# Four units of the second block's recurrent branch, computed in two parts around the end of the gather

## The reference

```python
# first block, last part: a product-key expert layer
u = expert_u[expert_idx]                       # 8 heads x 16 picks of 16384 experts, for each token
act = gelu(einsum('thkd,td->thk', u, hc))
vv = expert_v[expert_idx]
y = einsum('thk,thkd->td', gate * act, vv)
x = rmsnorm(x + y, final_g)
...
# second block, first part
h = rms_norm(x, norm_g)
p = h @ w_in                                   # its first 13 columns of tiles: r, k, v, w, a of the recurrent branch
r = p_r + (shifted p_r - p_r) * mu             # token_shift_mix, likewise for k, v, w, a
...
kv = rms_norm(mem, mem_norm_g) @ w_mem_kv      # memory keys and values
```

## Time and profile before

| | |
|---|---|
| median of 3 runs | 2595.02 us (2592.16 to 2595.42) |
| the profiled execution | 2597.78 us, span of its trace 2596.0 us |
| mean granted TensorE clock | 0.969 |
| busy, share of the span | PE 86%, PEld 54%, DVE 66%, ACT 33%, POOL 33% |
| gather stage | 571 to 1898 us of the span |
| first matmul of the second block | 1912.34 us |
| last of its 13 units done | about 1985.7 us |

### The profile page before, as it was taken

One profiled execution on the slowest core, in us unless ns is written; L12 is line 12 of the kernel. 1 busy time (PEld: TensorE's weight loads), 2 busy tenths in 40 slices (PEclk: granted clock), 3 DMA queues, 4 the chain that ended last, 5 costly groups with the idle time before them and its releaser, 6 DMA issues. The chain is left out here.

```text
span 2596.0 us, 33131 instructions
## 1 busy us (share of the span) xinstructions
PE 2229.3 (86%) x11846; PEld 1394.7 (54%) x11846; DVE 1703.7 (66%) x3855; ACT 866.8 (33%) x1931; POOL 864.0 (33%) x649
## 2 busy tenths in 40 slices
PE   8998999889987788877777777777779999989999
PEld 7886667765542333323332222223257777776787
DVE  7998797348676777766676667766544644456553
ACT  3222762333232342322232222322224222246431
POOL 0001213345444355534434344334313211212243
PEclk9999999999999999999999999999989999989999
DMA  4332215279999999999999999999922212232253
GB/s 146 106 110 94 78 50 179 73 267 414 421 421 419 421 420 419 413 421 415 419 417 418 417 409 417 415 408 411 420 74 90 85 62 73 88 126 94 84 196 106
DMA packets 131074, 682.50 MB, mean 263 GB/s; under 512 B 13536, under 2 KB 23136, under 8 KB 65120
## 3 DMA queue, kind: packets, MB, share of 16 engines
q0 software_dynamic: 73728, 536.90, 50.1%
q1 hardware_dynamic: 57184, 143.49, 15.8%
HBM read 655.70 MB, written 24.64 MB: 262 GB/s over the span
## 5 line engine op out<-in xcount | busy, mean ns | idle before, releaser
L1664 PE MATMUL bank<-peer_uv,peer_diag 128*128 128x512 f32 x2048 | 975.9, 622 | 284.6 <-ACT peer_diag L1323 279.6
L1557 DVE SCALAR_TENSOR_TENSOR peer_uv<-peer_uv,early_h 128x1024 f32<-128x1024 f32 x512 | 644.2, 1269 | 387.2 <-DMA peer_uv<-in_peer_uv,peer_index 382.9
L1664 PEld LDWEIGHTS bank<-peer_uv,peer_diag 128*128 128x128 f32 x2048 | 387.0, 197 | 834.4 <-issue 831.0
L1358 POOL DMA_INDIRECT peer_uv<-in_peer_uv,peer_index x512 | 535.1, 1045 | 742.9 <-PE bank L1664 654.0
L223 POOL TENSOR_TENSOR weight_low<-weight_ring,weight_high 128x1024 fp32r<-128x1024 f32 x102 | 248.8, 2439 | 680.3 <-ACT weight_high L206 680.3
L155 PE MATMUL bank<-hT_high,weight_high 128*128 128x512 f32 x952 | 403.0, 423 | 14.3 <-POOL weight_low L223 5.1
L156 PE MATMUL bank<-hT_low,weight_high 128*128 128x512 f32 x952 | 375.8, 395 | 0.0
L157 PE MATMUL bank<-hT_high,weight_low 128*128 128x512 f32 x952 | 375.3, 394 | 0.0
L206 ACT ACTIVATE weight_high<-weight_ring 128x1024 fp32r<-128x1024 f32 x171 | 180.9, 1058 | 468.9 <-PE bank L157 456.0
L1318 ACT ACTIVATE peer_gelu<-peer_dots 128x2 f32<-128x2 f32 x256 | 52.0, 203 | 798.3 <-DVE peer_uv L1557 798.2
L155 PEld LDWEIGHTS bank<-hT_high,weight_high 128*128 128x128 f32 x952 | 181.9, 191 | 66.5 <-issue 19.0
(11 more groups left out here) (416 smaller groups left out, 2740.0 us busy)
## 6 DMA issues: line engine op xcount, KB each, us to landing
weight_ring<-in_weights SPq DMA_DIRECT2D x171, 512.0 KB, 3.4
z_store<-fill_stage SPq DMA_DIRECT2D x70, 256.0 KB, 2.3
peer_uv<-in_peer_uv,peer_index POOLq DMA_INDIRECT x512
merge_z<-z_store SPq DMA_DIRECT2D x8, 768.0 KB, 6.0
merge_z<-z_store SPq DMA_DIRECT2D x12, 512.0 KB, 4.4
score_store<-peer_work SPq DMA_DIRECT2D x16, 192.0 KB
peer_sc<-score_store SPq DMA_DIRECT2D x24, 128.0 KB
swz<-z_store SPq DMA_DIRECT2D x1, 2560.0 KB, 9.5
```

Of the source, the lines that this page charges most:

```text
L1358: pool.indirect_dma_start(uv[:, p % SLOTS], None, peer_uv, bass.IndirectOffsetOnAxis(index[:, n % 2, p % TOPK:p % TOPK + 1], 0)).then_inc( ...
L1557: nc.vector.scalar_tensor_tensor(uv[:, p % SLOTS, 0:D], uv[:, p % SLOTS, 0:D], 1.0, h2[:, t], ALU.mult, ALU.mult, accum_out=dots[:, p % TO ...
L1664: mm = nc.tensor.matmul(bank[2 * (t % 2) + c][:], diag[:, p % SLOTS], uv[:, p % SLOTS, D + c * 512:D + (c + 1) * 512], start=(p % PICKS == ...
```

## The change

- SP loads the four first units of the recurrent branch (`r0` to `r0 + 3`) no longer in the gather but after the 254th of its 256 groups is summed. The store of the memory's keys and values is moved behind these loads; it no longer stands ahead of loads of scores.
- ACT makes the high parts of all four after the last group and before the last norm, two into `self.high`, two into a new buffer `more` that lies over tiles of `h2` that are no longer read. POOL makes the four low parts behind its last gather. The high and low parts of two of the units no longer lie in the gather.
- PE, behind the last group: units 0, 1 and 2 against the first 384 tokens into banks 4, 5, 6 (24 matmuls of 384 columns each), then `turn` of the last tile, then unit 3 into bank 7.
- In `rwkv_prepare` the four units are computed against the last 128 tokens (24 matmuls of 128 columns each) into the rest of the same banks; only then are they `done`, and the ring slots free. The other nine units are as before, except that the high parts of units 4 and 5 are made by ACT ahead of the copies of units 0 and 1.

```diff
@@ Weights
+    def place_more(self, offset):
+        self.more_offset = offset
+        self.more = same_place(self.nc, "weight_more", [P, 2, DT, P], offset)
@@ experts
+AHEAD, TURN_AFTER = 4, 3
+MORE_BEHIND_H2 = 960
@@ experts, SP
                 for k in range(DT):
-                    w.load(sp, m0 + RING + k + 1)
+                    w.load(sp, min(m0 + RING + k + 1, r0))
                     if k % 2:
                         scores(PH + 4 + k // 2)
-                for n in range(PH + 8, PH + 10):
+                for n in range(PH + 8, HEADS):
                     scores(n)
+
+                sp.wait_ge(summed, HEADS * GROUPS - 2)
+                w.load(sp, r0 + RING)
                 sp.wait_ge(kv_kept, 4)
                 sp.dma_start(mem_store, kv[:]).then_inc(kv_stored, 16)
-                for n in range(PH + 10, HEADS):
-                    scores(n)
                 sp.wait_ge(kv_stored, 16)
@@ experts, ACT
                     for k in range(DT):
-                        w.finished(act, m0 + k)
+                        if k < DT - 2:
+                            w.finished(act, m0 + k)
+                        else:
+                            act.wait_ge(w.done, m0 + k + 1)
...
+                for n in range(AHEAD):
+                    w.high_part(act, r0 + n, more=n >= 2)
                 for _ in norms(TT - 1):
                     pass
@@ experts, POOL
-                            QUERIES + 2 <= lows < QUERIES + DT + 2 and mem_group(lows - QUERIES - 2) + RINGS + 1 <= g):
+                            QUERIES + 2 <= lows < QUERIES + DT and mem_group(lows - QUERIES - 2) + RINGS + 1 <= g):
...
+                for n in range(AHEAD):
+                    w.low_part(pool, nc.gpsimd, r0 + n, more=n >= 2)
@@ experts, PE
-                turn(TT - 1)
+                pe.wait_ge(low_kept, DT * (TT - 1))
+                for n in range(AHEAD):
+                    if n == TURN_AFTER:
+                        turn(TT - 1)
+                    ring = w.wait(pe, r0 + n, more=n >= 2)
+                    for k in range(DT):
+                        product(nc, bank[4 + n][:, 0:T - P], ring[:, k], h3T[:, k, 0:T - P], k == 0, k == DT - 1)
@@ rwkv_prepare, PE
-                for n in range(UNITS):
+                for n in range(AHEAD):
+                    ring = w.wait(pe, u0 + n, more=n >= 2)
+                    for k in range(DT):
+                        mm = product(nc, bank[4 + n][:, T - P:T], ring[:, k], hT[:, k, T - P:T], k == 0, k == DT - 1)
+                    mm.then_inc(w.done, 1)
+                for n in range(AHEAD, UNITS):
                     ring = w.wait(pe, u0 + n)
-                    if n >= RING:
+                    if n >= AHEAD + RING:
                         pe.wait_ge(kept, n - RING + 1)
...
+                pe.wait_ge(kept, AHEAD)
                 then_fill(9)
@@ rwkv_prepare, ACT
                 for n in range(UNITS):
-                    w.finished(act, u0 + n)
-                    nc.scalar.activation(z[:, n, 1:T + 1], bank[n % RING][:], ACT.Copy).then_inc(kept, 1)
+                    act.wait_ge(w.done, u0 + n + 1)
+                    if n < 2:
+                        w.high_part(act, u0 + AHEAD + n)
+                    elif n >= AHEAD:
+                        w.high_part(act, u0 + n + 2)
+                    nc.scalar.activation(z[:, n, 1:T + 1], bank[4 + n if n < AHEAD else n % RING][:], ACT.Copy).then_inc(kept, 1)
```

More of the change, by code:

```diff
@@ L175, in __init__ @@
         self.issued = self.highs = self.lows = 0
+        self.more = None
+    def place_more(self, offset):
+        self.more_offset = offset
+        self.more = same_place(self.nc, "weight_more", [P, 2, DT, P], offset)
     def units(self, eng, start, upto, one):
@@ L200, in load, with high_part @@
         self.issued = upto
-    def high_part(self, act, u, i=0):
+    def high_part(self, act, u, i=0, more=False):
         if u < TOTAL:
             act.wait_ge(self.arrived[u % RING], 16 * i + 16 * (u // RING + 1))
-            self.nc.scalar.activation(self.high[:, u % 2].bitcast(F32R), self.ring[:, u % RING], ACT.Copy
+            self.nc.scalar.activation((self.more if more else self.high)[:, u % 2].bitcast(F32R), self.ring[:, u % RING], ACT.Copy
                                       ).then_inc(self.high_ready, 1)
@@ L226, in low_parts, with low_part, wait @@
         self.lows = self.highs = upto
-    def low_part(self, eng, vector, u):
+    def low_part(self, eng, vector, u, more=False):
         eng.wait_ge(self.high_ready, u + 1)
-        vector.tensor_tensor(self.low[:, u % RING].bitcast(F32R), self.ring[:, u % RING], self.high[:, u % 2],
+        vector.tensor_tensor(self.low[:, u % RING].bitcast(F32R), self.ring[:, u % RING], (self.more if more else self.high)[:, u % 2],
                              ALU.subtract).then_inc(self.split, 1)
         self.lows = u + 1
-    def wait(self, pe, u, i=0):
+    def wait(self, pe, u, i=0, more=False):
         pe.wait_ge(self.split, RING * i + (u + 1))
-        return Split(self.high[:, u % 2], self.low[:, u % RING])
+        return Split((self.more if more else self.high)[:, u % 2], self.low[:, u % RING])
 class Filler:
@@ L671, in first_block @@
         assert nc.sbuf_base - 4 * TT * D == attnT.high_offset
+        w.place_more(attnT.high_offset + MORE_BEHIND_H2)
         score_store = nc.dram_tensor("score_store", (TT, PH, P, 2, NKEYS), F32, kind="Internal").ap()
@@ L1156, in experts @@
         score_heads = score_store.rearrange("t h p e k -> p (t h) e k")
-        u0, m0 = first_unit("query"), first_unit("mem")
+        u0, m0, r0 = first_unit("query"), first_unit("mem"), first_unit("rwkv")
         x_turned, x_high, x_low, gained = (st.sem(n) for n in ("x_turned", "x_high", "x_low", "gained"))
@@ L1706, in second_block @@
     yaT, ya_offset = placed(nc, ctx, "yaT", [P, 4, T])
+    assert ya_offset == w.more_offset
     ya_low = same_place(nc, "yaT_low", [P, 4, T], ya_offset)
```

## The result

| | before | after |
|---|---|---|
| median of 6 runs each | 2593.69 us (2590.17 to 2598.54) | 2574.49 us (2570.52 to 2580.69) |
| ratio | | 0.9924, 95% interval 0.9907 to 0.9941 |
| the profiled execution | 2597.78 us | 2570.52 us, span 2568.7 us |
| mean granted TensorE clock | 0.969 | 0.976 |

The change makes the kernel 19.2 us faster; the forecast was 15.0. The runs of before beside it had a median 1.3 us lower than those the forecast started from, so the 1.0 us by which the range is missed is within the spread. The question is which microseconds of the gain the forecast did not have. The two profiled executions lie 27 us apart, because the one of before is among its slowest and the one of after is its fastest.

A forecast was written before the change was run, and what follows sets the result against it. DMA engines were taken to bound the gather (busy share 1.01). Gather 6.5 us less (7.5 - 1.0) and seam 8.5 less (29.8 against 38.3) made 15.0, so 2580.0 us, in a range from 2575.5 to 2590.

The forecast's parts named there:

- The bound and the gather: Gather: DMA engines are the bound, so four units and the store leaving it save 7.5 us by bytes.
- The 1.0 us for sharing with the late engine: Gather's end: the new loads share the late DMA engine with the last group, delaying it 0 to 2.5 us, taken 1.0.
- ACT, POOL and DVE: Seam: high parts end before the norm's first square; low parts may hold up DVE, tile ready at 8.2 to 13.0 us.
- TensorE in the seam: Last group to second block: start 0.3 us behind the group, four units of 384 columns 16.6 us, turn without wait; 18.2 us.
- the ring: Behind the seam: unit 4 waits for a free slot, load and split, 9.8 to 12.5 us, taken 11.3.
- A: 128-column split matmuls cost what plain f32 costs, 0.20 us each: gain 7.1 us, 2588; chance 0.20.
- C: Split format loses its speed already at 384 columns, 0.69 us a matmul: 42 us slower, 2637; chance 0.06.
- it fell only some 5 us into the idle time: Seam: PE's wait is too short for its clock to fall, since before it fell only some 5 us into idle time.
- in a fixed order, so a shift of unit 4 should shift the end by as much: After the seam: PE stands at nine tenths, so unit 4's earlier start reaches the kernel's end in full.
- B: Gather: the bytes saved do not show, as something else sets its end; gain 7.5 us, 2587.5; chance 0.07.
- D: Seam: weights land so late that PE idles over 5 us and unit 0 runs at 1.2 GHz; gain 7, 2588; chance 0.06.
- E: After the seam: the lead is given back in later waits, for instance at `mixed`; no gain, 2595; chance 0.05.

The follow-up runs named there:

- turn_after_4: The changed kernel with the last tile's turn behind all four units instead of three; 2586.06 us in one run.
- after_pad33: The changed kernel with 33 extra transposes of the identity on TensorE in gather groups 130 to 162; 2579.53 us, ratio 0.9942 to before.

## Why the prediction was right in its terms and wrong in its end

**The bound and the gather: right.** 7.5 us by bytes was the term, 7.7 the measured mean. The 1.0 us for sharing with the late engine was not there. The Trainium skill, "DMA: Bandwidth & Descriptors" (Queues, rings and completion order), says that an engine takes turns between its queues; by it up to 2.5 us could have been lost. The loads were issued at 1877.14, 0.8 us before the slices rise from 25 to 238 GB/s, and the last group's first dot product still starts 4.97 us behind that of the group before (1879.91 after 1874.94), as in before (1891.38 after 1886.41). No loss can be seen.

**ACT, POOL and DVE: right.** The fourth unit's high part ends at 1887.6, before the first square at 1888.40, so nothing queued behind is late. Of the two that read two SBUF tensors at once POOL paid, not DVE: its last two low parts took 5.75 us instead of 2 x 2.37, and the norm's tile was ready 8.5 us behind the group instead of 8.2. The forecast of 8.2 to 13.0 was too cautious and cost nothing.

**TensorE in the seam: right.** Start of the first unit 0.0 us behind the group (forecast 0.3); from there to the second block 18.07 (18.2); matmuls of 384 columns 0.173 us apart (0.173) and of 128 columns 0.111 (0.11); unit 4 at 11.2 us behind the block's start by the ring (11.3), 29.7 us in all (29.8). The short matmuls end only 0.3 us before it, so the ring and TensorE's own work nearly tie. So rivals A and C are out: the split format does not fall to the 0.20 and 0.69 us of plain f32. But 128 columns cost 0.111 us, twice their share of a 512-column matmul (0.227 / 4 = 0.057). The Trainium skill, "TensorE: Matmul & The Clock Gate" (LDWEIGHTS), has 107 ns for the weight load of 128 columns, which is near the 0.111; the 81 ns for a stream in its section Back-to-back issue gap are not reached here. The clock stayed up as forecast, since no wait was over 0.32 us, but the reason given ("it fell only some 5 us into the idle time") did not hold elsewhere: it fell 3.5 us into the idle time in `turn_after_4` (1908.3, idle from 1904.8), and just behind a wait of 1.70 us in `after_pad33`.

**The end: wrong.** The step that failed is "in a fixed order, so a shift of unit 4 should shift the end by as much". The order is fixed, but the change puts 190 instructions ahead of it, and where TensorE has to wait for instructions depends on their number. That is worth 5.5 us between the two kernels, in a stage that the change does not touch, and it was in neither the sum nor the range. Behind the core it seems to fail a second time, the other way: that stretch is some 3.5 us longer on average, by single traces. The low end of the range, 2575.5, had every known term near its best (the best case as added up, 8.5 + 1.8 + 10 = 20.3, would give 2574.7 and not 2576); the median came 1.0 us below the range with the known terms near the middle: 7.7 + 7.6 = 15.3 us by the means. So that 15.0 is no more than 4.2 us off is in part luck: the two unforeseen terms have opposite signs.

**Rivals B, D and E** fell too: the bytes show in full, TensorE was not idle behind the group, and the lead is not given back as a whole. A part of it seems to be, the 3.5 us behind the core.

What stays open: the runs show the period of 256 instructions, the places, the transfers that the pauses follow, and the price. Why the position half a block on costs no more than after's, why the burst at the same place is long in one execution and short in the next by some tenths, and what holds back the end by 3.5 us, they do not show.

## What to carry to other kernels

Where a hole in TensorE's work stands at the end of a stage bound by DMA, cutting a product along the tokens lets three quarters of it run before the last tile is ready; at the high clock 384 columns cost 0.173 us, in proportion, and 128 columns 0.111, twice their share, so the last quarter is not free. Keep a long piece for the last wait before the short ones. Here the next unit then started by a ring without slack, and a late load cost up to 3 us (`after_pad33`). When a change adds or takes instructions of TensorE, compare the waits named "issue" in the later fast bursts as well: moving work can be worth some microseconds there, in either sign, and a padding of a few harmless instructions in idle time tells that part from the rest. And take a stage's length from several executions before a difference of 0.3% is explained.

## What was not expected of the hardware

- Pauses of up to 1.8 us of TensorE within bursts, at a multiple of 256 instructions plus 192, that end 1.06 to 1.60 us after a transfer of 16.4 kB of instructions has landed; 11.0 us of the core in before, 6.8 in after.
- After a wait of 3.69 us the granted clock stayed at 0.50 for over 20 us of fully busy TensorE, through all 96 matmuls of 128 columns, and came back within the first 512-column unit. In the seam of before, the unit that began at low clock was back at 0.22 us a matmul after 5.9 us.
- At the end of the gather the rate is down to about one engine's: 25 to 41 GB/s for 6 us in after, 20 to 31 in before. Loads issued beside it cost the last group nothing that can be seen.
